# Input projection of the short-convolution layer: eight half-block products per pair, or seven

## The reference

```python
def short_conv_mixer(a, w_in, conv_w, w_out):
    gate_b, gate_c, u = jnp.split(a @ w_in, 3, axis=-1)
    return (gate_b * dwconv3(gate_c * u, conv_w)) @ w_out
```

## Time and profile before

| | us |
|---|---|
| median of 3 runs | 2996.56 (2992.07 to 2998.43) |
| the profiled execution | 2993.15 |
| its span | 2991.4 |
| stage `scin` | 2430.6 to 2564.8 of the span |
| stage `scout` | 2564.8 to about 2609.7 |
| mean granted TensorE clock | 0.987 |

### The profile page before, as it was taken

One profiled execution on the slowest core, in us unless ns is written; L12 is line 12 of the kernel. 1 busy time (PEld: TensorE's weight loads), 2 busy tenths in 40 slices (PEclk: granted clock), 3 DMA queues, 4 the chain that ended last, 5 costly groups with the idle time before them and its releaser, 6 DMA issues.

```text
span 2991.4 us, 46812 instructions
## 1 busy us (share of the span) xinstructions
PE 2913.9 (97%) x19658; PEld 2583.3 (86%) x19658; DVE 1797.0 (60%) x2666; ACT 1300.3 (43%) x2153; POOL 483.1 (16%) x405
## 2 busy tenths in 40 slices
PE   6998999999999999999999999999999999999999
PEld 6997887899999999999999977667888878788887
DVE  7776664579597453547949757655535543465453
ACT  4575664344243455644424445654323332343231
POOL 0002221123032000002303313001202111121020
PEclk9998997999999999999999999999999999999999
DMA  2210000245554321025545520102232222223232
GB/s 103 89 53 36 2 2 6 75 156 183 170 170 164 113 88 36 1 79 183 176 164 189 188 99 29 43 17 83 94 97 88 97 90 93 91 85 101 90 97 86
DMA packets 79554, 284.34 MB, mean 95 GB/s; under 512 B 8528, under 2 KB 9296, under 8 KB 78576
## 3 DMA queue, kind: packets, MB, share of 16 engines
q1 hardware_dynamic: 79344, 281.35, 28.1%
HBM read 274.96 MB, written 6.36 MB: 94 GB/s over the span
## 4 chain that ended last, share of the span: by engine, by line
PE 93%; DVE 4%; ACT 2%; issue 1%; POOL 1%; DMA 0%; SPq 0%; DVEq 0%; ACTq 0%
PE psum L348 67%; PE psum L2733 2%; PE psum L1893 2%; PE psum L912 2%; PE psum L2104 2%; PE psum L2086 1%; PE psum L2077 1%; PE psum L1269 1%; PE psum L848 1%; PE psum L539 1%; PE psum L1319 1%; PE psum L1286 1%; PE psum L2430 1%; PE psum L2727 1%; PE psum L2721 1%
## 5 line engine op out<-in xcount | busy, mean ns | idle before, releaser
L303 DVE TENSOR_TENSOR wlo<-wraw,whi 128x1024 fp32r<-128x1024 f32 (+2 forms) x398 | 507.7, 1297 | 614.7 <-ACT whi L296 605.8
L296 ACT CAST whi<-wraw 128x1024 fp32r<-128x1024 f32 (+2 forms) x398 | 396.3, 1021 | 495.2 <-PE psum L348 460.6
L431 DVE CUSTOM_DVE_ANT_0 araw<-araw,cond 128x1024 f32<-128x1024 f32 x112 | 181.1, 1654 | 0.0
L348 PE MATMUL psum<-f0xh,whi 128*128 128x264 f32 x704 | 143.1, 285 | 0.0
L348 PE MATMUL psum<-f0xh,wlo 128*128 128x264 f32 x704 | 143.0, 285 | 0.0
L348 PE MATMUL psum<-f0xl,whi 128*128 128x264 f32 x704 | 142.4, 284 | 0.0
L348 PE MATMUL psum<-f1xh,whi 128*128 128x258 f32 x704 | 141.9, 283 | 0.0
L348 PE MATMUL psum<-f1xh,wlo 128*128 128x258 f32 x704 | 141.9, 283 | 0.0
L348 PE MATMUL psum<-f1xl,whi 128*128 128x258 f32 x704 | 141.4, 282 | 0.0
L348 PE MATMUL psum<-f2xh,whi 128*128 128x512 f32 x352 | 139.1, 395 | 1.0 <-DVE f2xl L592 1.0
L348 PE MATMUL psum<-f3xh,whi 128*128 128x512 f32 x352 | 139.1, 395 | 1.0 <-DVE f3xl L592 1.0
(11 more groups left out here) (515 smaller groups left out, 8193.9 us busy)
## 6 DMA issues: line engine op xcount, KB each, us to landing
wraw<-d_w SPq DMA_DIRECT2D x357, 512.0 KB, 3.4
araw<-d_ada SPq DMA_DIRECT2D x112, 512.0 KB, 3.3
wraw<-d_w SPq DMA_DIRECT2D x32, 384.0 KB, 3.6
hn<-d_h SPq DMA_DIRECT2D x4, 528.0 KB, 7.9
hres<-d_h SPq DMA_DIRECT2D x1, 2112.0 KB, 8.2
spill<-hres SPq DMA_DIRECT2D x1, 2112.0 KB, 7.4
hres<-spill SPq DMA_DIRECT2D x1, 2112.0 KB, 8.5
cond<-d_cond SPq DMA_DIRECT2D x2, 1024.0 KB, 4.8
```

What stands on the lines that cost most here:

```text
L296: e.copy(whi[0:rows, n % NH, 0:kt * cols], wraw[0:rows, n % NR, 0:kt * cols]).then_inc(*w_hi.up(n))
L303: e.tensor_tensor(wlo[0:rows, n % NH, 0:kt * cols], wraw[0:rows, n % NR, 0:kt * cols], whi[0:rows, n % NH, 0:kt * cols].bitcast(F32), ALU. ...
L348: ins = e.matmul(psum[0:bw, b0 + nb * len(sl) + si, 0:ln], l_ if z == 2 else h_, (xp.lo if z == 1 else xp.hi)[:, k, o:o + ln], start=k == ...
L431: e.tensor_tensor_reduce(out=w, in0=w, in1=self.c[:, col, :], scale=1.0, scalar=0.0, op0=ALU.mult, op1=ALU.add, accum_out=ada[:, ly, blk, ...
```

## The change

Pairs 2 to 11 of `scin` are computed by Strassen's scheme, one level, in the form that shares partial sums. The two by two blocks are: weights by (first or second 4 k-tiles) x (first or second output block), activations by (k-tiles 0 to 3 or 4 to 7) x (tokens 0 to 255 or 256 to 511). Seven products of 4 k-tiles x 128 outputs x 256 tokens take the place of eight. Pairs 0 and 1 go through `lin_pe` as before.

```diff
+def by_seven(tag, j):
+    ...
+    return tag == "scin" and "sc" in SEVEN and j >= PLAIN
```

The three places of `whi` and `wlo` become six half places. A plain chunk takes two; a pair by seven has seven items `(n, 0)` to `(n, 6)`, each the weight factor of a product, one half place each. Item 0 is a quarter of the raw weights, as are 2 + 1 and others after GpSimd has written sums over them:

```diff
         def w_dma(e, n):
             _, _, _, kt, rows, cols = PLAN[n]
-            if n >= NR:
-                e.wait_ge(*w_lo.at(n - NR))
+            m = n - NR
+            if m >= 0:
+                tag, j, k, *_ = PLAN[m]
+                if not by_seven(tag, j):
+                    e.wait_ge(*w_lo.at(m))
+                elif k == 0:
+                    e.wait_ge(*w_lo.at(m, 4))
+                    e.wait_ge(*w_sum.at(m, 3))
+                else:
+                    e.wait_ge(*w_lo.at(m - 1, 6))
...
+        def factor_of(n, i):
+            return (quarter(n, 0), pair_sum(n), quarter(n, 1), quarter(n + 1, 0), quarter(n, 0), quarter(n + 1, 1),
+                    quarter(n + 1, 0))[i]
...
+                e.scalar_tensor_tensor(out=w_place(wlo, n, i), in0=factor_of(n, i), scalar=1.0,
+                                       in1=w_place(whi, n, i).bitcast(F32), op0=ALU.mult,
+                                       op1=ALU.subtract).then_inc(*w_lo.up(n, i))
...
+        def w_sum_pool(e, n, s):
+            if s == 0:
+                ...
+                e.tensor_tensor(pair_sum(n), quarter(n, 0), quarter(n, 1), ALU.subtract).then_inc(*w_sum.up(n, 0))
+            elif s == 1:
+                raw_here(e, n + 1)
+                e.wait_ge(*w_sum.at(n, 0))
+                e.tensor_tensor(quarter(n, 1), quarter(n + 1, 1), pair_sum(n), ALU.subtract).then_inc(*w_sum.up(n, 1))
+            elif s == 2:
+                e.wait_ge(*w_sum.at(n, 1))
+                e.wait_ge(*w_lo.at(n, 0))
+                e.tensor_tensor(quarter(n, 0), quarter(n, 1), quarter(n, 0), ALU.add).then_inc(*w_sum.up(n, 2))
+            else:
+                e.wait_ge(*w_lo.at(n, 3))
+                e.tensor_tensor(quarter(n + 1, 0), quarter(n + 1, 0), quarter(n, 1), ALU.subtract).then_inc(*w_sum.up(n, 3))
```

Casts of items 1, 2, 4 and 6 wait for `w_sum` 0, 1, 2 and 3. TensorE's part; banks b to b + 3 change between two sets of four:

```diff
+        def seven_pe(e, n, b, X, ready):
+            ...
+            steps = [(b, plain(0, first)), (b + 3, turned(2)), (b + 1, turned(3)), (b, plain(4, first)), (b + 2, turned(0)),
+                     (b + 1, turned(1)), (b + 2, plain(4, second))]
+            for i, (bank, operand) in enumerate(steps):
+                e.wait_ge(*w_lo.at(n, i))
+                ready(e, i)
+                wh, wl = w_place(whi, n, i), w_place(wlo, n, i)
+                for k in range(4):
+                    for z in range(3):
+                        ins = e.matmul(psum[:, bank, 0:half], (wl if z == 2 else wh)[:, k, :], operand(z, k),
+                                       start=i < 2 and k == 0 and z == 0, stop=k == 3 and z == 2, skip_group_check=True)
+                ins.then_inc(*w_used.up(n, i))
```

`ready` waits before product 2 for ScalarE's copy of bank b to b + 1, before product 4 for its copy of b + 1 to b + 2, and before product 6 for VectorE's `added(j, 1)`. ScalarE also copies bank b + 3 to SBUF (`Sc.p7`). In the loop over pairs:

```diff
+            def added(j, h):
+                ...
+                if h:
+                    e.wait_ge(*y_cp.at(j, 7))
+                e.wait_ge(*w_used.at(scin_chunk(j), 4 if h else 5))
+                e.tensor_tensor(to, psum[:, bank, 0:half], Sc.p7[:, j % 2, :], ALU.add).then_inc(*y_ad.up(nb, h))
+                if part == 2:
+                    if h:
+                        e.wait_ge(*part_made(nb - 1))
+                    e.wait_ge(*y_ad.at(nb, h))
+                    e.tensor_tensor(to, to, gcc[:, i, cols[h]], ALU.mult).then_inc(*y_u.up(blk, h))
...
+            for j in range(PLAIN, 12):        # VectorE
+                ...
+                w_freed(e, w_split_dve, *AHEAD[(n, 0)])
+                for i in range(3):
+                    w_freed(e, w_split_dve, n, i)
+                    if there is not None:
+                        tap(there, i)
+                if nb % 3 == 2:
+                    e.wait_ge(*w_used.at(n, 3))
+                    product(nb // 3, 0, b)
+                w_freed(e, w_split_dve, n, 3)
+                added(j, 1)
+                w_freed(e, w_split_dve, n, 4)
+                added(j, 0)
+                w_freed(e, w_split_dve, n, 5)
```

`w_freed(..., n, i)` splits the item six places on: after product 0 the pair's own item 6, after 1 to 5 the next pair's items 0 to 4, at the head of the loop item 5. `there` is the convolution block whose third input was made in the pair before; `product` is the old L2951 in halves. GpSimd in its loop:

```diff
+            for j in range(PLAIN, 13):
+                there = next((x // 3 for x in (2 * j - 2, 2 * j - 1) if x % 3 == 2), None)
+                if j < 11:
+                    for s in (0, 1, 2):
+                        w_sum_pool(e, scin_chunk(j + 1), s)
+                if there is not None:
+                    ...
+                    e.tensor_tensor(cc, cc, gb[:, i, :], ALU.mult).then_inc(*y_m.up(there))
+                if j < 11:
+                    w_sum_pool(e, scin_chunk(j + 1), 3)
+                if there is not None:
+                    ...
```

More of the change, by code:

```diff
@@ L316, in splits_ahead @@
             for n, _, _ in chunks_of(tag, j):
-                split(e, n + NH - 1)
+                w_freed(e, split, *AHEAD[(n,)])
         class Pair:
@@ L1642, in __init__ @@
                 self.freed = []
-                for half in range(2):
+                for half in range(2 * (f not in SEVEN)):
                     self.freed += [f_u.at(f, 22 * half + 2 * j + 1) for j in range(11)]
@@ L2867, in program @@
         sc0 = mem.lo
[L2868 removed]
+        scrt = mem.left("scrt", [128, LX])
         mem.lo = sc0
@@ new lines, in sc_act, with part_to, plain_out @@
+            norm_act(e, "sc", shift, Sc.nt, xc, slice(0, LX))
+            half = LX // 2
+            first, second = slice(0, half), slice(half, LX)
+            def part_to(nb):
+                blk, part = divmod(nb, 3)
+                if blk >= 3:
+                    e.wait_ge(*(u_made(blk - 3) if part else y_m.at(blk - 3)))
+                return (gcc if part else gb)[:, blk % 3, :]
+            def plain_out(nb):
+                e.activation(part_to(nb), psum[:, nb, 0:LX], ACT.Copy).then_inc(*y_e.up(nb, 1))
@@ new lines, in hidden, with behind @@
+            def hidden(blk):
+                e.wait_ge(*y_m.at(blk))
+                e.copy(xo3.hi[:, blk, :], co_[:, blk % 3, :]).then_inc(*y_hi.up(blk))
+            def behind(j):
+                nb = 2 * j
+                if j < PLAIN:
+                    e.wait_ge(*w_used.at(last_chunk("scin", j)))
+                    for x in (nb, nb + 1):
+                        if x in AC:
+                            plain_out(x)
+                elif nb in AC:
+                    e.wait_ge(*w_used.at(scin_chunk(j), 6))
+                    e.activation(part_to(nb)[:, second], psum[:, scin_bank(j) + 2, 0:half], ACT.Copy).then_inc(*y_e.up(nb, 1))
@@ L2929, in sc_act @@
+            behind(11)
+            hidden(7)
             splits_and_squares(e, "scout", sq_f3)
@@ new lines, in product @@
+            def product(blk, h, bank):
+                i = blk % 3
+                if h == (0 if (3 * blk + 2) >= 2 * PLAIN else 1):
+                    e.wait_ge(*part_made(3 * blk + 1))
+                if 3 * blk + 2 < 2 * PLAIN:
+                    e.tensor_tensor(cu_[:, i, 1:LX + 1], psum[:, bank, 0:LX], gcc[:, i, :], ALU.mult).then_inc(*y_u.up(blk, 1))
+                else:
+                    e.tensor_tensor(cu_[:, i, up[h]], psum[:, bank, 0:half], gcc[:, i, cols[h]], ALU.mult).then_inc(*y_u.up(blk, h))
@@ L2963, in sc_pool @@
+            for i in range(3):
+                tap(7, i)
+            add_dve(e, "scout", "scout", x2, LX, gate=adv(1, 2), set0=2)
         def sc_pool(e):
             rms_add(e, "sc", sqx)
+            turn_first(e, "sc", Sc, lambda a, b: ada[:, 1, a:b, 0])
+            turn_sums(e, "sc", Sc, 0)
+            turn_sums(e, "sc", Sc, 1)
+            w_sum_pool(e, scin_chunk(PLAIN), 0)
             e.wait_ge(*n_lov.at("sc", 7))
```

386 lines of the change are left out of this document (294 added, 92 removed).

## The result

The changed kernel takes 3018.8 us (median of 12 runs, 3005.8 to 3023.3), the kernel before 2998.5 us beside it (12 runs, 2992.1 to 3008.3). The ratio is 1.0061, with a 95% interval of 1.0047 to 1.0075: slower by 0.6%, about 20 us. The forecast was 3014, with a range of 2990 to 3030.

The account below looks back on a forecast made before the run. The prediction took TensorE, busy for 97% of the span, to bound the kernel: -13.3 us (matmuls) + 23.5 (lateness) + 5 (start) + 3 (clock) = +18, against the median 2996.56, forecast 3014 us, range 2990 to 3030.

Parts of the forecast that it names:

- The start: GpSimd's turned sums and a weight sum fall in the norm ahead of `scin`: 5 us, bounds 0 and 9.
- A: Pairs 2, 5, 8, whose second block is a convolution input: product 6 starts 1.5 us late.
- Lateness: Product 6 waits for `added` in the pairs of seven products: 7.8 us per three pairs, 23.5 for nine.
- B: Pairs 3, 6, 9: second chunk's load goes out late, so `added` and product 6 come 5.2 us late.
- C: Pairs 4, 7, 10: `added` ends at 9.5 us into the pair, product 6 is 1.1 us late.
- The taking of turns: VectorE's two-SBUF-input and GpSimd's operations alternate in `scin`: 1.69 us for one of each, 35.1 us per three pairs.
- The clock: Stalls in pairs 3, 6, 9 put TensorE's following matmuls at half clock: 3 us, bounds 0 and 8.
- the hold: In pairs 2, 5, 8 `added` keeps VectorE waiting for product 6's evacuation, with the splits for products 3 and 4 behind.
- the late load: In pairs 3, 6, 9 the second weight chunk's load goes out at 5.0 us and lands at 8.4, delaying its sum.
- Rival 1: Faster: GpSimd's sums in `scin` fall where VectorE waits or reads PSUM; 2988 us, chance 0.18.
- Rival 2: Even: the load lands before it is needed and B falls to C's level; about 2997 us, chance 0.13.
- Rival 3: Heavier: GpSimd blocked twice per operation or half clock throughout the stalls; 3031 us, chance 0.14.

Follow-up runs that it names:

- e8: Changed kernel with GpSimd's turned sums and first weight sum held until the norm's end, behind the memsets of `cu_` edges; stage 155.3 us against 154.0.
- e1: Changed kernel with each GpSimd weight sum replaced by two memsets of about its length that read nothing; stage 130.2 us against 154.0.
- e3: Changed kernel with the product of the convolution's second half moved out of `added` to the next pair; 3011.1 us, ratio 1.0039 to the kernel before.
- e5: Changed kernel with the edits of e3 and e4 together; 3010.0 us, ratio 1.0038 to the kernel before.
- e4: Changed kernel with a fourth raw weight buffer, so a pair's second chunk loads a pair earlier; 3015.5 us, ratio 1.0056 to the kernel before.
- e6: Changed kernel with GpSimd's turned sums held until the norm's end and the memsets of `cu_` edges behind them; stage 157.4 us against 154.0.
- e2: Changed kernel with each GpSimd weight sum replaced by one memset of 8 columns, 0.10 us; stage 133.1 us against 154.0.

## Why the prediction was right

By its terms, in the profiled execution (stage 154.0 - 134.5 = +19.5 us):

- **Matmuls**: 840 of 117.7 ns and 96 of 233.3 make 121.3 us, 13.1 less than the 134.4 of before; predicted 13.3. Right, and the 0.2 are my rounding: 84 times 117.8 ns is 9.90 us and not 9.87.
- **The start**: pairs 0 and 1 lost 4.7 us, predicted 5, and e8 shows that it was the port. But "just make pair 2" was wrong: pair 2 waited 4.2 us at product 6 where I had given it A's 1.5, with the turned halves and the sums asking for the port together; in e1, where the sums read nothing, pair 2 has no wait.
- **Lateness**: 20.1 us measured, 23.5 predicted. A was 1.3 (predicted 1.5), B 4.9 in pairs 6 and 9 and 3.6 in pair 3 (5.2), C nothing (1.1). C was over-counted. That VectorE catches up in B's stall is my reading; e3 speaks for it, where B is 3.3 and C has its 1.0 us, but no run was made to test it. The taking of turns, and its 35.1 us for three pairs, is borne out by the 34.3 to 34.7 us in which the port was in use, and by e3 and e5, where three pairs take 35.6 to 36.1. VectorE's operations with a PSUM input, 3.3 us for three pairs, stand outside that sum; they fit beside GpSimd's turns.
- **The clock**: I took 3 us. In the changed kernel 71 matmuls (26 behind pair 2's stall, 15 behind each of three others) ran 213 ns apart, 71 x 0.0956 = 6.8 us. The granted clock was the lower one behind each of the four stalls of 3.6 us or more. A stall of B cost 1.4 us and not 2, but C swallowed nothing of it, and the prediction had nothing for pair 2, whose stall cost 2.5. This term was mis-sized by 3.8 us, the lateness by 3.4 the other way. (The Trainium skill, TensorE: Matmul & The Clock Gate, section Back-to-back issue gap, gives N/1.2 for the lower clock, 213.3 ns at 256 columns; the trace agrees.)
- **The rest**: 1.1 us of short waits. Sum: -13.1 + 4.7 + 20.1 + 6.8 + 1.1 = +19.6, against +18 on record. That it comes so near is in part luck: the errors of the lateness and of the clock cancel.
- **The end** cost nothing, as predicted: from `scout`'s first matmul to its last it is 44.6 us before and after.

One step failed in its reasoning, though not in its size: the cause of B. I had put B's 5.2 us on the hold, and from there on the late load and sum s = 1. The trace seemed to confirm it: in pair 6 that sum begins 8.4 us into the pair, as in my walk, and `added` ends at 13.2. Half of it stands: without the hold (e3) B falls from 4.9 to 3.3 us. The load does not: e4 took its wait away, 16.0 to 1.3 us, and B stayed. What remains in B goes with the backlog of VectorE itself: the port is in use for 34.4 us in three pairs, while TensorE wants 29.6. My walk followed one chain, and a second of the same length lay beside it.

Rival 1 (faster, 2988) fell with the splits at 1109 ns. Rival 2 (B falls to C's level once the load is early) was put to the test by e4, where the load was early and B did not fall. Rival 3 came true in the clock alone.

## What to carry to other kernels

Before work is given to GpSimd to relieve TensorE, add up per round what VectorE's operations with two SBUF inputs and GpSimd's reading operations ask of the port that they share, and compare the sum with TensorE's time for the round: here 11.7 us against 9.9, where VectorE's own sum was some 8 and GpSimd's 6.9. Where the sum is too large, do the trick in every second round, and only once the preparations are paid for: seven products in four pairs gain 0.15%, in ten they lose 0.6%. A wait for a load that the trace shows need not be worth anything; give it a buffer and look whether the next engine was late too.

## What I had not expected of the hardware

- The lower clock need not be there when TensorE starts again. Of the 24 stalls of 3.3 us or more in the stage over all these runs, 23 were followed by matmuls at half rate, but the granted clock fell anywhere from within the stall to 1.4 us behind its end (e5, pair 6), after matmuls at full rate. Then 12 to 18 matmuls of 256 columns ran at 213 ns, or 24 to 27 (in e6 once 13 of 512 columns): 1.1 to 2.6 us on top of the stall.
- The length of the stall alone does not settle it. One of 3.32 us in e3 (pair 6) was followed by none, one of 3.29 us in the same run by 17; of the four between 2.0 and 2.1 us (three in e2, one in e6) one was, in e2, 1.5 us after its end. Below 2.0 us there was none.
- I had counted one VectorE operation in the way of each of GpSimd's. In pair 6 line 398 took 2.29 us where a sum undisturbed takes 1.29: it began under a tap, and a split followed at 2513.8 us before it was done.
